# Hybrid decoder layer: the conv branch's norm moved to the residual addition, its last products placed around the first head's scores

## What is computed

```python
h  = x + W_out[ concat( DiffAttn(rmsnorm(x)), ShortConv(rmsnorm(x)) ) ]
x' = h + HierMoE(rmsnorm(h))
...
def diff_attention(q, k, v, lam, lambda_init, subln_gain):   # 4 heads, q blocks of 128 rows
    ...
        p = jax.nn.softmax(s, axis=-1)
        a = p[:, :, 0] - lam * p[:, :, 1]
    ...
    o = rms_norm(o, subln_gain) * (1.0 - lambda_init)        # per head, over its 128 columns
def short_conv(cb, cc, cu, conv_w, out_gain):
    y = cc * cu
    ...
    z = sum(conv_w[j] * yp[:, j:j + seq] for j in range(CONV_K))
    return rms_norm(cb * z, out_gain)                        # over the 512 conv columns
```

## Time and profile before

| | before |
|---|---|
| median of 3 runs | 1189.92 us (1189.32 to 1190.0) |
| profiled execution | 1192.26 us |
| its span in the trace | 1190.5 us |
| PE, PEld busy | 1111.0 us (93%), 872.3 us (73%) |
| DVE, ACT, POOL busy | 846.8, 659.7, 349.2 us |
| data moved | 254.16 MB |

### The profile page before, as it was taken

The page is one execution under the profiler, slowest core; times in us unless marked ns, Lnnn a source line. Parts: engine busy times, 40 slices in busy tenths (PEclk is TensorE's granted clock), DMA queues, the critical chain, the costliest instruction groups (busy, mean ns, idle before and its releaser), DMA issues.

```text
span 1190.5 us, 15280 instructions
## 1 busy us (share of the span) xinstructions
PE 1111.0 (93%) x5645; PEld 872.3 (73%) x5645; DVE 846.8 (71%) x1117; ACT 659.7 (55%) x909; POOL 349.2 (29%) x432
## 2 busy tenths in 40 slices
PE   4999999999769999988879999999999999999995
PEld 3998989898658787777757777777777777766673
DVE  6634353443487667766749899898899889888893
ACT  5412121211366545544338778778778778777783
POOL 2432333232321111112103442443443443322220
PEclk9999999999789999999789999999999999999998
DMA  8011030300410212322699999999999999999972
GB/s 242 16 56 51 18 89 1 92 16 18 177 24 19 89 71 90 124 104 92 231 313 331 376 369 376 375 364 375 378 375 371 375 363 358 370 373 359 373 307 41
DMA packets 76506, 254.16 MB, mean 213 GB/s; under 512 B 17808, under 2 KB 42384, under 8 KB 51856
## 3 DMA queue, kind: packets, MB, share of 16 engines
q1 hardware_dynamic: 69264, 236.37, 53.5%
q0 software_dynamic: 7168, 16.79, 6.0%
HBM read 240.55 MB, written 20.97 MB: 220 GB/s over the span
## 4 chain that ended last, share of the span: by engine, by line
PE 42%; DMA 7%; DVE 3%; ACT 1%; issue 1%; POOL 0%; POOLq 0%; DVEq 0%; ACTq 0%
PE banks L2070 9%; PE banks L2072 9%; PE banks L2071 8%; PE banks L2087 4%; PE banks L2089 4%; PE banks L2091 4%; DMA raw<-in_w_up 3%; DMA raw<-in_w_gate 3%; PE banks L2046 2%; DVE wlo L1991 1%; DMA rows<-xn_rows,table_i 1%; PE banks L2055 1%; ACT whi L1940 1%; DMA out<-y_sb,table_i 0%; DVE hn L1193 0%
## 5 line engine op out<-in xcount | busy, mean ns | idle before, releaser
L1991 DVE TENSOR_TENSOR wlo<-raw,whi 128x2048 fp32r<-128x2048 f32 x190 | 427.7, 2286 | 50.1 <-ACT whi L1940 49.8
L1940 ACT CAST whi<-raw 128x2048 fp32r<-128x2048 f32 x188 | 354.1, 1911 | 34.6 <-DMA raw<-in_w_gate 20.2
L2070 PE MATMUL banks<-whi,rT_hi 128*96 128x512 f32 x512 | 206.8, 404 | 6.1 <-DVE wlo L1991 5.0
L1922 POOL DMA_INDIRECT out<-y_sb,table_i x32 | 152.2, 4758 | 197.8 <-ACT y_sb L1958 192.7
L2072 PE MATMUL banks<-whi,rT_lo 128*96 128x512 f32 x512 | 202.9, 396 | 0.0
L2071 PE MATMUL banks<-wlo,rT_hi 128*96 128x512 f32 x512 | 201.8, 394 | 0.0
L2070 PEld LDWEIGHTS banks<-whi,rT_hi 128*96 128x96 f32 x512 | 83.1, 162 | 40.6 <-DVE wlo L1991 6.1
L2072 PEld LDWEIGHTS banks<-whi,rT_lo 128*96 128x96 f32 x512 | 82.9, 162 | 36.4
L2071 PEld LDWEIGHTS banks<-wlo,rT_hi 128*96 128x96 f32 x512 | 83.4, 163 | 31.5 <-issue 0.5
L1913 POOL DMA_INDIRECT rows<-xn_rows,table_i x30 | 50.7, 1691 | 188.7 <-PE banks L2046 173.5
L847 ACT ACTIVATE qk_sq<-banks 128x256 f32<-128x256 f32 x32 | 12.3, 384 | 155.7 <-PE banks L1470 155.7
(11 more groups left out here) (250 smaller groups left out, 2035.4 us busy)
## 6 DMA issues: line engine op xcount, KB each, us to landing
raw<-in_w_gate SPq DMA_DIRECT2D x64, 1024.0 KB, 22.1
raw<-in_w_up SPq DMA_DIRECT2D x64, 1024.0 KB, 22.1
raw<-in_w_down SPq DMA_DIRECT2D x64, 1024.0 KB, 23.3
c_raw<-in_w_in SPq DMA_DIRECT2D x12, 512.0 KB, 3.8
q_raw<-in_w_in SPq DMA_DIRECT2D x12, 512.0 KB, 5.8
x_stage<-in_x SPq DMA_DIRECT2D x8, 512.0 KB, 7.9
wo_raw<-in_w_out SPq DMA_DIRECT2D x2, 2048.0 KB, 10.1
h_sb<-in_x SPq DMA_DIRECT2D x8, 512.0 KB, 4.6
```

The costliest lines, as they stand in the source:

```text
L1922: pool.indirect_dma_start(out=s.out_rows, out_offset=bass.IndirectOffsetOnAxis(ap=s.table_i[:, e:e + 1], axis=0), in_=s.y_sb[e % 2][:], in ...
L1940: act.copy(s.w_hi[i % HI][:], s.raw[i % RING][:]).then_inc(s.hi_ready, 1)
L1991: dve.tensor_tensor(s.w_lo[i % RING][:], s.raw[i % RING][:], s.w_hi[i % HI][:].bitcast(F32), ALU.subtract).then_inc(s.lo_ready, 1)
L2070: pe.matmul(o, s.rT_hi[e % 2][:, c, :], hi[:, c4, :], start=(c == 0), stop=False)
```

## The change

The conv branch goes unnormed into the output product. Its gain, a number per channel, is multiplied into rows 512 to 1023 of W_out as they are split (`conv_taps[:, m, 3]`). Its root, a number per token, multiplies the whole product where x is added: h = rstd_c * (conv + attention) + x. The attention half has to be divided by that root first: POOL's step for the attention row's norm, (sum + eps), is multiplied by `inv_var` = 1 / (conv mean + eps) before its power -1/2. The diagonal matrices, the spread and the eight scalings are gone. DVE makes `inv_var` in one step more. `sum_conv` stands in slot 1 behind `weigh(0)`, no longer in slot 0.

Unit 22 stands after piece 31. Unit 23 is cut into two halves of 12 matmuls: the first after the transposes of k 30 and of q 0, the second behind the scores of slot 0. `score` waits only for the k, bank reads and b takes that it needs. `double_q` 0 and 1 stand ahead of `square_bz` on POOL, and POOL's conv root stands in slot 2, ahead of `rstd_o(0)`.

```diff
-UNIT_AFTER = (-1, 2, 5, 6, 7, 7, 9, 11, 13, 14, 15, 15, 17, 19, 21, 22, 23, 23, 25, 26, 28, 29, 30, 31)
+UNIT_AFTER = (-1, 2, 5, 6, 7, 7, 9, 11, 13, 14, 15, 15, 17, 19, 21, 22, 23, 23, 25, 26, 28, 29, 31, 31)
...
-            sp.wait_ge(conv_ready, 2 * CT)
+            sp.wait_ge(conv_mean, 1)
...
             def rstd_o(g):
                 c = slice(g % 2, g % 2 + 1)
                 pool.wait_ge(o_squared, g + 1)
-                own.then(pool.tensor_tensor(s.o_rstd[:, c], s.o_ss[:, c], s.eps_o[:], ALU.add))
+                t = tile_head(g)[0]
+                own.then(pool.tensor_scalar(s.o_rstd[:, c], s.o_ss[:, c], s.eps_o[:], s.inv_var[:, t:t + 1], ALU.add, ALU.mult))
...
+                if p == PROJ - 1:
+                    double_q(0)
+                    double_q(1)
                 for n in units_after(p):
                     if unit(n)[1] == "b":
                         square_bz(n)
...
-            double_q(0)
-            double_q(1)
             for g in range(SLOTS_2):
-                if g == 0:
+                if g == 2:
                     pool.wait_ge(conv_mean, 1)
                     pool.tensor_tensor(s.rstd_c[:], s.rstd_c[:], s.neg_half[:], ALU.pow).then_inc(conv_rstd, 1)
...
-                if g == 0:
-                    spread_rstd()
...
-                    act.copy(s.wo_hi[:, k, :], s.wo_raw[:, k, :]).then_inc(wo_hi_ready, 1)
+                    if k >= CT:
+                        act.activation(s.wo_hi[:, k, :], s.wo_raw[:, k, :], ACT.Identity,
+                                       scale=s.conv_taps[:, k - CT, 3:4]).then_inc(wo_hi_ready, 1)
...
-            def scale_conv():
-                dve.wait_ge(rstd_spread, 1)
-                for half in range(2):
-                    for m in range(CT):
-                        z = s.mixC[:, m, half_cols(half)]
-                        dve.scalar_tensor_tensor(z, z, s.conv_taps[:, m, 3:4], ps[:, 6 + half, :], ALU.mult, ALU.mult).then_inc(conv_ready, 1)
...
-                dve.tensor_tensor(h, ps[:, 6 + n, :], h, ALU.add).then_inc(h_ready, 1)
+                if i == 0:
+                    dve.wait_ge(conv_rstd, 1)
+                dve.scalar_tensor_tensor(h, ps[:, 6 + n, :], s.rstd_c[:, TILES[i]:TILES[i] + 1], h, ALU.mult, ALU.add).then_inc(h_ready, 1)
...
+                if g == 0:
+                    take_b(UNITS - 1)
                 mix(g)
...
-                if g == 0:
+                if g == 1:
                     dve.wait_ge(conv_summed, 1)
-                    dve.tensor_scalar(s.rstd_c[:], ps[:, 7, 0:NT], 1.0 / CONV, EPS, ALU.mult, ALU.add).then_inc(conv_mean, 1)
-                if g == 2:
-                    scale_conv()
+                    do(dve.tensor_scalar(s.rstd_c[:], ps[:, 7, 0:NT], 1.0 / CONV, EPS, ALU.mult, ALU.add))
+                    dve.reciprocal(s.inv_var[:], s.rstd_c[:]).then_inc(conv_mean, 1)
...
+                    if k >= CT:
+                        dve.scalar_tensor_tensor(s.wo_lo[:, k, :], s.wo_raw[:, k, :], s.conv_taps[:, k - CT, 3:4],
+                                                 s.wo_hi[:, k, :].bitcast(F32), ALU.mult, ALU.subtract).then_inc(wo_lo_ready, 1)
...
+            multiply_unit(UNITS - 2)
             turn_k(PROJ - 2)
+            turn_q(0)
+            multiply_unit(UNITS - 1, (0,))
             turn_k(PROJ - 1)
-            turn_q(0)
-            turn_q(1)
             for g in range(SLOTS_2):
                 score(g, 0)
...
                 if g == 0:
-                    sum_conv()
-                if g == 2:
-                    spread_rstd()
+                    turn_q(1)
+                    multiply_unit(UNITS - 1, (1,))
...
                 if g >= 1:
                     weigh(g - 1)
+                if g == 1:
+                    sum_conv()
```

71 lines of the change are left out of this document (35 added, 36 removed).

## The result

The first comparison gave 1183.28 us (1181.1 to 1184.69, 6 runs) for the changed kernel against 1189.96 us (1189.32 to 1195.2, 6 runs) for the kernel before: a ratio of 0.9932, 95% interval 0.991 to 0.9955. The medians lie 6.7 us apart; the ratio, which isn't that of the medians (0.9944), stands for 8.1 us. The same changed kernel was run twice more beside the kernel before.

| comparison | before | changed | ratio | interval | gain by medians | gain by the ratio |
|---|---|---|---|---|---|---|
| first | 1189.96 (6 runs) | 1183.28 | 0.9932 | 0.991 to 0.9955 | 6.7 us | 8.1 us |
| second (e1) | 1192.5 (17 runs) | 1182.46 | 0.9917 | 0.9892 to 0.9943 | 10.0 us | 9.9 us |
| third (e9) | 1192.71 (11 runs) | 1183.08 | 0.9915 | 0.9897 to 0.9934 | 9.6 us | 10.1 us |

The account below looks back on a forecast made before the run. Bound: a chain of hand-offs between engines from the last conv product to attention, not TensorE work. 11.4 - 0.9 - 0.3 + 0.3 = 10.5 us off the median 1189.92 gave 1179.4 us, range 1176.0 to 1183.0.

Parts of the forecast that it names:

- The last units: Unit 22 still ends at 300.78, split unit 23 at 308.5; score inputs ready, the 2.14 us gap hidden under unit work.
- Mark 1: Turn of the third query (query 2) at 312.2 against 320.04, 7.8 us won, with a new idle stretch of 3.7 us.
- Mark 2: Turn of query 3 at 318.9 against 324.83, 5.9 us won; clock falls in the gap, back before sum_conv's 1.9 us.
- (a): Rival: clock stays at 1.2 GHz through sum_conv; 8.3 us won, 1181.6 us; chance 0.14.
- (b): Rival: clock doesn't fall at all in the 3.7 us gap; 13 us won, 1176.9 us; chance 0.14.
- Mark 3: VectorE's start on head 3 at 327.2 against 338.59, 11.4 us won; mix of head 2 at 323.1.
- (c): Rival: VectorE's four low-half steps of w_out run at half throughput, 4.6 us back, 1184.0 us; chance 0.03.
- The costs in later slots: GpSimd's pointer step, 0.1 us more per head, costs 0.9 us; the addition of x from PSUM costs 0.3 us.
- (e): Rival: slower, GpSimd's pointer step long in each head; 0.41 us more per step eats the gain; 1194 us; chance 0.05.
- The clock, "0.3 us won": A shorter gap before head 1's output, about 3.4 us for 8.34, may leave the clock higher: 0.3 us won.
- The shift reaches the end whole: Everything behind the stretch hangs on it through waits alone, so the whole shift was expected at the end.
- (d): Rival: gain absorbed, later slots wait for something unmoved, such as the router weights' load; about 1189 us; chance 0.04.

Follow-up runs that it names:

- e1: The changed kernel again without edit, beside the kernel before: 1182.46 us, ratio 0.9917.
- e9: The changed kernel once more without edit, beside the kernel before: 1183.08 us, ratio 0.9915.
- e2: Kernel before with only the norm moved to the addition of x; unit order, waits and queues as before: 1187.76 us, ratio 0.9955.
- e3: Kernel before with only the new order of units, queries, sum_conv and conv root, norm unmoved: 1190.11 us, ratio 0.9979.
- e4: Changed kernel with GpSimd's copies of queries 2 and 3 ahead of the squares of unit 23: 1175.96 us, ratio 0.9865.
- e6: Changed kernel plus 16 unused matmuls of 512 columns behind unit 23, filling TensorE's gap before query 2: 1181.08 us, ratio 0.9899.
- e7: Changed kernel with GpSimd's conv root moved behind the first attention root: 1183.1 us, ratio 0.9917.
- e5: Changed kernel with GpSimd's attention norm step without the inverse multiplication, output scaled wrongly, a timing alone: 1181.1 us, ratio 0.9899.

## Why the prediction was right in the gain and wrong in the time

**What bounds the stretch: right.** The marks came within 0.65 us of where they were put, and e2 and e3 show that the scalings and the order each carry a share. The shift forecast for VectorE's start on head 3 was 11.4 us; it is 11.2 us counted from the same point of both executions.

**The last units: right.** 308.5 forecast, 308.59 measured; the scores' inputs were ready, and the old gap of 2.14 us is gone.

**Mark 1: right, with a size off.** 312.5 for 312.2. Behind VectorE's wait for unit 23 stood the mix of head 0; it took 1.25 us instead of 0.75 us, beside GpSimd's squares, and was covered, as argued. e4 shows that this cover is real: once the query doesn't wait for the squares, the mix is the next gap.

**Mark 2: the mechanism was right, the size 0.65 us short.** The clock fell in the gap, and it was back for `sum_conv` (1.8 us between starts, 1.9 forecast), so neither (a) nor (b) happened. But the work up to `sum_conv` took 5.23 us instead of 4.79: I took the distance from the earlier trace rows, and the slow part of it was longer here. That the half clock would cost something here was in the sum; that it costs 2.2 us and goes when the gap is filled is what e6 showed. I named (b) with 2.5 us for a clock that doesn't fall; its price was nearly right.

**Mark 3: right.** 4.2 us to the mix of head 2 was 3.8; from there to VectorE's next query 4.1 us was 4.25. The 0.3 us for the conv root ahead of the first attention root is the 0.31 us of e7. The wait for ScalarE's rounding was taken as 0.3 us and is 0.32. The two low halves take 2.48 us, 1.28 each:

```profile
L1394 DVE SCALAR_TENSOR_TENSOR wo_lo<-wo_raw,conv_taps,wo_hi 128x1024 fp32r<-128x1024 f32 x4 | 5.0, 1282 | 0.3 <-ACT wo_hi L1014 0.3
```

So rival (c) fell. The rule of the Trainium skill behind it ("Vector Engine (DVE) Microarchitecture Reference", "Points that are easy to get wrong") isn't what this row shows: 1282 ns with two such sources, 1218 ns for the tensor_tensor of the earlier trace rows.

**The costs in later slots: both sizes off, one against the other.** GpSimd's step costs 0.155 us more and not 0.1. By my count of 10 waits that would have been 1.6 us; it is about 0.7 (e5): the waits between 350 and 560 us, which I counted, moved the last head by 0.2 us, and the first two heads, which I didn't count, by more. That the figure of 0.9 us comes near is luck: the step was taken too small and its reach too wide. The addition of x had no row of its own:

```profile
L1176 DVE SCALAR_TENSOR_TENSOR h_sb<-banks,rstd_c,h_sb 128x512 f32<-128x512 f32 x16 | 11.9, 743 | 0.0
```

743 ns for the 682 ns of the earlier trace rows, 0.06 us more, 16 times, 1.0 us of VectorE's time where I bounded it with 0.5. The error is one of reading: 5.35 us for eight scalings is the distance between starts of instructions that overlap, and 682 ns is the duration of one. The two don't compare. What the 1.0 us does to the end wasn't tried on its own, but e5 has this addition and not the pointer, and against the kernel before its lead stays at 10.0 to 10.1 us from head 4 to head 12 and at 10.2 us from head 25 to 31, stretches in which the two show the same distances from root to root. There the addition costs 0.1 us or less, where the sum had 0.3. Rival (e), with 0.41 us more per step as its point of decision, was far away.

**The clock, "0.3 us won": wrong.** The first stretch did become warmer (0.90 for 0.76 over 300 to 350 us), but behind the gap of 1.9 us in slot 5, which no edit touches, the clock was low in two of three executions of this kernel and in six of all twelve, and 1.5 us went there each time. The gap's length didn't decide it. Such steps, up or down, are larger than any term for the later slots, and I had no place for them in the sum.

**The shift reaches the end whole: nearly.** 11.0 us at the start of head 3, 9.2 at the gather, 9.1 at the end. The expert stage kept its length (599.9 us from the gather to the end in both). (d) didn't happen: the router weights were issued from 321.0 to 326.7, landed at most 5.5 us later, and GpSimd read them first, at 338.7.

**The step that failed: the subtraction from the median of three.** The time of the kernel before was taken as 1189.92 us, from runs of 1189.32 to 1190.0. Over 17 and 11 later runs its median is 1192.5 and 1192.71, with single runs from 1188.77 to 1195.01. The profiled execution, 1192.26, was the typical one, and I had set it aside as 2.3 us over the median. Starting from it the same sum gives 1181.8, and from 1192.5 it gives 1182.0; the changed kernel took 1182.46, 1183.08 and 1183.28. So of the miss of 3.9 us, 2.3 to 2.8 are the start; the rest is within what one step of the clock takes (1.5 us between the roots of heads 3 and 4 in the profiled execution). The range had the same fault: it was made around the sum's terms alone, with nothing for the 3 us by which two executions of one kernel differ. (a), (b) and (c) were forecast within 5 us of the main forecast, so the whole time alone couldn't have told them apart; the marks in the trace did.

Still open: why the first comparison had the kernel before at 1189.96 us and the others at 1192.5 to 1192.9. Each comparison was made apart from the others, the later ones on three different chips, and the first one's chip isn't on record, so another chip isn't ruled out. Plain chance isn't either: four of the first six runs lie at 1189.3 to 1190.0 and two at 1193.2 and 1195.2, and single runs below 1190 occur in two of the three later sets as well. No trace of an execution near 1189.5 us is there to show where it passed at full clock.

## What to carry to other kernels

When a long per-token or per-channel scaling stands between a producer and a chain of hand-offs, look for the linear step behind which it can be applied at little cost, and then look again at what the freed result was forcing into place: here a quarter of the gain (2.7 of 11.2 us) came only from moving the norm and the order together. After such a change read the new gap's releaser, not its length: an in-order queue that does deferrable work (squares) ahead of a ready input (the query copy) was worth about 4 us more in the trace and 3 to 7 in the whole times, for two moved copies. And take the start of a sum from enough runs; with a spread of 6 us a median of three may be off by more than the terms that one argues about.
